# Decay rows of a gated delta rule: sixteen broadcast products, or one product and a transfer through memory

## The reference, cut to what matters

```python
beta = jax.nn.sigmoid(b)
g = -jnp.exp(A_log) * jax.nn.softplus(a + dt_bias)
g_cum = jnp.cumsum(to_chunks(g), axis=-1)
decay = jnp.exp(jnp.where(causal, g_cum[..., :, None] - g_cum[..., None, :], -jnp.inf))
m = jnp.where(strict, jnp.einsum('bhnid,bhnjd->bhnij', k_beta, kc) * decay, 0.0)
attn_intra = jnp.einsum('bhnid,bhnjd->bhnij', qc, kc) * decay
```

## Time and profile before

| | us |
|---|---|
| median of 3 runs | 906.03 |
| lowest, highest | 905.59, 906.92 |
| span of the profiled execution | 905.7 |
| TensorE busy | 894.0 (99%) |
| VectorE busy | 604.6 (67%) |
| ScalarE busy | 456.3 (50%) |
| POOL busy | 95.4 (11%) |

### The profile page before, as it was taken

One profiled execution on the slowest core, in us unless ns is written; L12 is line 12 of the kernel. 1 busy time (PEld: TensorE's weight loads), 2 busy tenths in 40 slices (PEclk: granted clock), 3 DMA queues, 4 the chain that ended last, 5 costly groups with the idle time before them and its releaser, 6 DMA issues.

```text
span 905.7 us, 12742 instructions
## 1 busy us (share of the span) xinstructions
PE 894.0 (99%) x5426; PEld 761.5 (84%) x5426; DVE 604.6 (67%) x723; ACT 456.3 (50%) x554; POOL 95.4 (11%) x94
## 2 busy tenths in 40 slices
PE   8999999999999999999999999999999999999997
PEld 8989888788888887888888878778788888888885
DVE  5899896676566557778857564655556566664665
ACT  6675564564444447555443355443355555444443
POOL 2041231100000000000126310110100000000000
PEclk9999999999999999999999999999999999999999
DMA  9654324246555543654564544344454356445531
GB/s 331 248 205 147 126 63 170 88 163 230 198 194 198 197 190 140 221 186 149 208 221 167 185 159 167 140 186 184 171 200 142 141 194 234 171 183 216 186 140 46
DMA packets 26088, 160.45 MB, mean 177 GB/s; under 512 B 3576, under 2 KB 4232, under 8 KB 8240
## 3 DMA queue, kind: packets, MB, share of 16 engines
q1 hardware_dynamic: 23616, 153.40, 46.3%
q0 software_dynamic: 2272, 6.24, 2.1%
q10 hardware_dynamic: 144, 0.00, 0.0%
HBM read 158.57 MB, written 2.63 MB: 178 GB/s over the span
## 4 chain that ended last, share of the span: by engine, by line
PE 81%; DVE 13%; ACT 3%; issue 2%; DMA 1%; POOL 0%; POOLq 0%; SPq 0%; DVEq 0%; ACTq 0%
PE banks L501 33%; PE banks L469 21%; PE banks L472 10%; DVE t_wl L1620 5%; PE banks L573 3%; PE banks L529 2%; PE banks L424 2%; PE banks L443 2%; PE banks L1019 2%; DVE t_cout L1649 2%; PE banks L412 1%; PE banks L765 1%; ACT t_wh L1139 1%; PE banks L969 1%; PE banks L1101 1%
## 5 line engine op out<-in xcount | busy, mean ns | idle before, releaser
L1620 DVE TENSOR_TENSOR t_wl<-t_raw,t_wh 128x2048 fp32r<-128x2048 f32 x136 | 312.4, 2318 | 117.0 <-ACT t_wh L1139 115.8
L469 PE MATMUL banks<-t_hx,t_wh 128*128 128x512 f32 x992 | 312.0, 396 | 0.0
L1139 ACT CAST t_wh<-t_raw 128x2048 fp32r<-128x2048 f32 x136 | 255.6, 1907 | 12.3 <-DMA t_raw<-in_W 7.6
L472 PEld LDWEIGHTS banks<-t_hx,t_wl 128*128 128x128 f32 x992 | 186.3, 188 | 43.7
L472 PE MATMUL banks<-t_hx,t_wl 128*128 128x256 f32 x992 | 194.9, 278 | 0.0
L469 PEld LDWEIGHTS banks<-t_hx,t_wh 128*128 128x128 f32 x992 | 153.3, 189 | 2.4
L501 PE MATMUL banks<-t_wh,t_hx 128*128 128x512 f32 x320 | 102.0, 395 | 0.0
L501 PEld LDWEIGHTS banks<-t_wh,t_hx 128*128 128x128 f32 x320 | 59.5, 188 | 12.7 <-issue 0.6
L501 PE MATMUL banks<-t_wl,t_hx 128*128 128x512 f32 x160 | 61.1, 390 | 0.0
L2251 POOL TENSOR_TENSOR t_st<-t_st,t_half 128x1 f32<-128x1 f32 (+1 forms) x18 | 10.6, 591 | 435.5 <-DVE t_st L1649 425.8
L1471 ACT COPY t_hold<-banks 128x512 f32<-128x512 f32 x28 | 16.4, 585 | 67.4 <-PE banks L472 56.2
(11 more groups left out here) (322 smaller groups left out, 1340.4 us busy)
## 6 DMA issues: line engine op xcount, KB each, us to landing
t_raw<-in_W SPq DMA_DIRECT2D x139, 1024.0 KB, 4.8
t_raw<-in_W SPq DMA_DIRECT2D x8, 256.0 KB, 6.5
t_raw<-in_W SPq DMA_DIRECT2D x4, 512.0 KB, 8.8
skew<-scr POOLq DMA_DIRECT2D x1, 1536.0 KB, 13.0
t_cout<-in_xT SPq DMA_DIRECT2D x4, 256.0 KB, 5.6
t_x<-in_x SPq DMA_DIRECT2D x2, 512.0 KB, 9.7
t_tab<-in_tab POOLq DMA_DIRECT2D x1, 640.0 KB, 7.4
out<-t_xt SPq DMA_DIRECT2D x2, 320.0 KB, 2.3
```

What stands on the lines that cost most here:

```text
L469: e.matmul(bank[b + c], M.wh[:, h, wk], M.hx[:, k, :, :].rearrange("p a s -> p (a s)"), start=k == 0, stop=False)
L472: m = e.matmul(bank[b + c][:, 0:S], M.wl[:, h, wk], M.hh[:, k, :], start=False, stop=k == 7)
L1139: e.copy(M.wh[:, h, :], M.raw[:, r, :]).then_inc(q.sem, q.tick(("hi", i)))
L1620: e.tensor_tensor(M.wl[:, h, :], M.raw[:, r, :], M.wh[:, h, :].bitcast(F32), ALU.subtract).then_inc(q.sem, q.tick(("lo", i)))
```

## The change

The 16 products and their four banks go. In their place TensorE makes one product with `graw` as the stationary side, 16 partitions by 128 columns, which is g_cum along the columns for each of the 16. ScalarE copies it to SBUF (`grow`, in a free part of the tile `va`), in unit 3 ahead of the first silu. POOL writes it to memory (gscr, 8 KB), waits, and loads `dU` from it, 16 rows of 512 bytes to each of 128 partitions, 1 MB; this stands behind the issue of skew and ahead of the first T loads. VectorE's 16 operations move from the end of unit 3 to unit 5, behind rn1 and ahead of the low part of unit 8, and work in place on `dU` in SBUF; they wait for the load. The product with `nstrict` (dS) moves from VectorE to POOL, behind the powers rk and rq and ahead of kd.

```diff
--- before.py
+++ after.py
@@ -307,6 +307,7 @@
             M.T = sb(pa, "T", [128, 2, 384])
             M.oh, M.ng = M.PT[0:32, 0, :], M.PT[0:8, 1, :]
             M.rb, M.rrow = M.va[0:32, 0, 0:8], M.va[0:8, 1, 0:384]
+            M.grow = M.va[0:16, 0, 128:256]
 
             def four(own, other):
                 return [own[:, 0, :], own[:, 1, :], other[:, 0:384], other[:, 384:768]]
@@ -364,7 +365,7 @@
         PE, AC, DV, PO = (Line(top.enter_context(nc.semaphore(n + "_done"))) for n in ("pe", "act", "dve", "pool"))
         raw_in = [top.enter_context(nc.semaphore(f"raw_in{i}")) for i in range(RR)]
         LD = {n: top.enter_context(nc.semaphore("in_" + n)) for n in (
-            "x0", "x1", "small", "ident", "tab", "onehot", "neg", "rbT", "scr", "skew", "post_mix", "post_mlp",
+            "x0", "x1", "small", "ident", "tab", "onehot", "neg", "rbT", "scr", "skew", "gscr", "dU", "post_mix", "post_mlp",
             "dist", "rope", "g_final", "pre", "wab", *(f"T{h}" for h in range(8)), *(f"xT{p}" for p in range(4)),
             *(f"W{i}_{p}" for i, n in PIECES.items() for p in range(n - 1)))}
         s_out = top.enter_context(nc.semaphore("out_written"))
@@ -662,15 +663,11 @@
                     e.matmul(bank[b][:, 0:16], M.triu, M.graw, start=True, stop=True)
                     e.matmul(bank[b][:, 16:32], M.ones, M.graw, start=True, stop=True).then_inc(q.sem, q.tick("sums"))
                     drain(b, DV, "kdx0")
-                    for g in range(4):
-                        b = take(("decay", g), g)
-                        opened(b)
-                        for i in range(4):
-                            s = 4 * g + i
-                            m = e.matmul(bank[b][:, i * 128:i * 128 + 128],
-                                         M.graw[:, s:s + 1].broadcast_to([128, 128]), M.triu, start=True, stop=True)
-                        m.then_inc(q.sem, q.tick(("decay", g)))
-                        drain(b, DV, ("dU", g))
+                    b = take("rows", 0)
+                    opened(b)
+                    e.matmul(bank[b][0:16, 0:128], M.graw, M.triu, start=True, stop=True).then_inc(
+                        q.sem, q.tick("rows"))
+                    drain(b, AC, "grow")
 
             c_block("z", x_in, [(AC, ("zz", t)) for t in range(2)])
             b_unit(("qk", 0), DV, ("qk", 0), to=0)
@@ -1283,6 +1280,8 @@
                     e.activation(M.cout[:, a, :], M.cin[:, a, 0:S], ACT.Copy,
                                  scale=cw[:, a, 0:1]).then_inc(q.sem, q.tick(("tap", a, 0)))
                 if u == 3:
+                    q.wait_ge(PE, "rows")
+                    e.copy(M.grow, bank[at["rows"]][0:16, 0:128]).then_inc(q.sem, q.tick("grow"))
                     silu_of(0)
                     silu_of(1)
                     silu_of(2)
@@ -1304,7 +1303,7 @@
                 q.wait_ge(PO, ("rstd", "in", c))
                 e.activation(M.zz[:, c, :], bank[at["z", c]][:], ACT.Silu, scale=M.ms[:, c:c + 1]).then_inc(
                     q.sem, q.tick(("zz", c)))
-            q.wait_ge(DV, ("dU", 3))
+            q.wait_ge(DV, "dU")
             e.activation(M.dU[:], M.dU[:], ACT.Exp).then_inc(q.sem, q.tick("dexp"))
             q.wait_ge(DV, "gc")
             e.activation(M.eg, M.gcum, ACT.Exp).then_inc(q.sem, q.tick("eg"))
@@ -1783,6 +1782,9 @@
                     q.wait_ge(q, "rn0")
                     ts(rq, rq, EPS, 64.0, ALU.add, ALU.mult, "rn1")
                     ts(rk, rk, EPS, None, ALU.add, None, "rn1")
+                    q.wait_dma(LD["dU"])
+                    for s in range(16):
+                        stt(M.dU[:, s, :], M.dU[:, s, :], M.gcum[:, s:s + 1], M.cap, ALU.subtract, ALU.min, "dU")
                     next_unit()
                 for k in range(1, 4):
                     for i in range(2):
@@ -1796,13 +1798,6 @@
                     e.tensor_copy(M.gcum, bank[b][:, 0:16]).then_inc(q.sem, q.tick("gc"))
                     q.wait_ge(q, "gc")
                     tt(M.kdx, bank[b][:, 16:32], M.gcum, ALU.subtract, "kdx0")
-                    for g in range(4):
-                        b = at["decay", g]
-                        q.wait_ge(PE, ("decay", g))
-                        for i in range(4):
-                            s = 4 * g + i
-                            stt(M.dU[:, s, :], bank[b][:, i * 128:i * 128 + 128], M.gcum[:, s:s + 1], M.cap,
-                                ALU.subtract, ALU.min, ("dU", g))
 
             q.wait_ge(PO, "rk")
             for c in range(2):
@@ -1822,8 +1817,6 @@
                 tt(M.kTa[:, 2 * u:2 * u + 2, :], halves(bank[at["qk", u]][:]), rep(M.rbc, 2), ALU.mult, ("qk", u))
 
             keys(0)
-            q.wait_ge(AC, "dexp")
-            tt(M.AT, M.dU[:], rep(M.nstrict, 16), ALU.mult, "dS")
             next_unit()
             next_unit()
             keys(1)
@@ -1862,7 +1855,7 @@
                 v = bank[at["KQ", g]][:].rearrange("p (i w n) -> p i w n", i=2, w=2)
                 a_, du = M.AT[:, s0:s0 + 3:2, :], M.dU[:, s0:s0 + 3:2, :]
                 q.wait_ge(PE, ("KQ", g))
-                q.wait_ge(q, "dS")
+                q.wait_ge(PO, "dS")
                 tt(a_, v[:, :, 0, :], a_, ALU.mult, ("AT", g))
                 tt(du, v[:, :, 1, :], du, ALU.mult, ("dq", g))
             next_unit()
@@ -2286,12 +2279,18 @@
             e.dma_start(A["scr"], M.rrow).then_inc(LD["scr"], 16)
             q.wait_dma(LD["scr"])
             e.dma_start(A["skew"], bass.AP(A["scr"].tensor, 0, [[384, 8], [0, 128], [1, 384]])).then_inc(LD["skew"], 16)
+            q.wait_ge(AC, "grow")
+            e.dma_start(A["gscr"], M.grow).then_inc(LD["gscr"], 16)
+            q.wait_dma(LD["gscr"])
+            e.dma_start(M.dU[:], bass.AP(A["gscr"].tensor, 0, [[0, 128], [128, 16], [1, 128]])).then_inc(LD["dU"], 16)
             load_T(0)
             load_T(1)
             q.wait_ge(DV, "rn1")
             for w, name in ((1, "rk"), (0, "rq")):
                 o = M.rn.rearrange("p (c w h) -> p c w h", c=2, w=2)[:, :, w, :]
                 tt(o, o, M.half[:, 0:16].rearrange("p (c h) -> p c h", c=2), ALU.pow, name)
+            q.wait_ge(AC, "dexp")
+            tt(M.AT, M.dU[:], rep(M.nstrict, 16), ALU.mult, "dS")
             q.wait_ge(AC, ("kT", 1, 2))
             q.wait_ge(AC, "kdx")
             tt(heads(M.kd), heads(M.tm[:, 0, 512:1024]), bc(M.kdx[:, 0:8], 64), ALU.mult, "kd")
@@ -2459,6 +2458,7 @@
     nc = bacc.Bacc("TRN2", target_bir_lowering=False, num_devices=1)
     A = {n: nc.dram_tensor("in_" + n, a.shape, F32, kind="ExternalInput").ap() for n, a in arrays.items()}
     A["skew"] = nc.dram_tensor("skew", [8, 128, 384], F32, kind="Internal").ap()
+    A["gscr"] = nc.dram_tensor("gscr", [16, 128], F32, kind="Internal").ap()
     A["scr"] = nc.dram_tensor("scr", [8, 384], F32, kind="Internal").ap()
     out = nc.dram_tensor("out_0", (S, D), F32, kind="ExternalOutput").ap()
     build(nc, A, out)
```

## The result

The changed kernel took 908.51 us (median of 21 runs, 906.65 to 908.81), the kernel before 906.40 (21 runs, 905.10 to 908.10). The ratio is 1.0020, 95% interval 1.0013 to 1.0026: slower by 1.2 to 2.4 us. The forecast was +0.9 us, with a range of 904.8 to 910.8.

The account below looks back on a forecast made before the run. The chain was taken to run through VectorE up to the last convolution taps, then ScalarE's exponential and unit 10's split, not TensorE. Only VectorE's idle counted, +0.9 us on the 906.03 median: 906.9, range 904.8 to 910.8.

Parts of the forecast that it names:

- late load: Rival: VectorE waits for dU's load before the sixteen operations, each us past 57.1 costing one; 910.3 to 912.2; chance 0.26.
- Part 1: TensorE, sixteen products become one: of 3.4 us it keeps 1.2 at unit 4, and is 1.6 ahead after unit 5.
- Part 2: VectorE's sixteen operations, moved behind unit 5's norm sums and reading SBUF, still take 4.14 us; floor 2.1 us less.
- Part 3: VectorE's order without the sixteen operations: idle 0.6 and 0.25 us, last taps at 63.45 instead of 62.55, +0.9 us.
- second gap: VectorE idle 0.25 us near 51.5, waiting for TensorE's unit 5 before scaling.
- Parts 4 and 5: Mask product on POOL takes 8.2 to 9.2 us, slows VectorE's low parts by a third; costed at nothing, at most 0.5.
- The prediction's rival: POOL's product holds VectorE whole, delaying low parts 10 and 11 and TensorE's third score products 3 us: 910; chance 0.06.
- Part 6: Rows through memory: write landed at 46.7, load 9.5 us more, landing at 56.2, 0.9 before VectorE asks; ends 51.6, 62.4.
- the middle price: Load of dU priced by the T loads at 49 ns a row: 9.5 us, landing 0.9 us before VectorE asks.
- The sum's base: The +0.9 us was added to the profiled span of 905.7; the median of three runs, 906.03, lay 0.3 above it.

Follow-up runs that it names:

- the first profile: The changed kernel unaltered, its first profiled execution, a run of 906.80 us; median 908.51 against 906.40 for the kernel before.
- after_filled: The changed kernel plus eight idle 128x128 products of constants in TensorE's hole in front of unit 4: 907.16 us against 906.36 before, ratio 1.0010.
- after_again: The changed kernel unaltered, timed and profiled a second time: 908.11 us against 906.41 for the kernel before, ratio 1.0018.
- ds_vector: The changed kernel with the mask product (dS) back on VectorE: 907.89 us against 906.41 for the kernel before, ratio 1.0012.
- load_late: after_filled with POOL's write and load of the rows behind the four T loads: 912.67 us against 906.33 for the kernel before, ratio 1.0067.

## Why the prediction was right, and where it was not

**The sign, the chain and the place of the cost** were right: nothing was gained from TensorE's 3.6 us and VectorE's 2.2 us, and the chain ran over the last taps, the exponential and unit 10's high part to the transposes. Ahead of them it ran over VectorE, as the prediction has it, only where the clock held; with the fall it ran over TensorE's units 4 and 5. The measured change, 1.2 to 2.4 us with 2.1 between the medians, is at the edge of the 0.2% that the forecast called no change, and more than twice its 0.9. That 908.51 still lies in the range is luck: the range reached to 910.8 for a late load, which did not happen, and had nothing in it for what did.

**Part 1** was right in its numbers: 1.2 us kept by unit 4 (36.51 - 27.56 = 8.95 against 39.17 - 29.00 = 10.17), the wait for dU's banks gone. It failed in leaving the hole that these numbers imply, 35.8 to 37.95, unpriced. It costs 1.48 us in the executions in which the clock falls. This is the term that the sum lacked, and most of the difference to the measurement: 0.75 from the first profile, and with the 1.48 of the fall 2.2, against 2.1 measured. after_filled agrees that little else is needed: without the hole it is +0.80, and the forecast, which had no term for the hole, was +0.9.

**Part 2** was right: 4.21 us by the spacing, from SBUF, for 4.14 from PSUM.

**Part 3** was right in kind and a little high: 0.51 and no second gap, for 0.6 and 0.25. Unit 5 was done just as VectorE came (no idle time at 50.06). In after_again this second gap is the one that grew to 1.46 with the slow clock. Of the hole in front of unit 8 (0.96) the prediction says nothing; there TensorE is off the chain in the first profile and it cost no time.

**Parts 4 and 5** had the wrong mechanism and, by luck, nearly the right cost. Between the Trainium skill's rule of an exclusive lock and my reading of the earlier trace rows I believed the reading, and the rule was right. I had taken the POOL products for 2.05 us each, from a row of two. Taken with the ends, the first took 1.0, the low part then its 2.2 until 126.70, and the second 0.9 behind that until 127.61: the same lock. So 2048 columns take POOL 4.4 us, not 8.2 to 9.2, and hold VectorE for as long as they last. The prediction had two errors here, contention in place of a hold and a product twice too long, and they offset each other. The prediction's rival priced the hold with 8.7 us, at +3 us; with 4.4 it is 0.1 here and 0.9 where the kernel before has no slack. The score products did not wait for POOL.

**Part 6** was right that the load is hidden, though not in its two prices: the write took 4.7 to 7.3 us to land in nine profiles and the load 5.3 to 8.1, against 4.6 and 9.5. The two errors cancel, which is luck too. In five profiles the load landed 3.2, 0.7, 0.2, 1.5 and 1.2 us before VectorE asked, where the middle price left 0.9. The estimate by the fit of the Trainium skill ("DMA: Bandwidth & Descriptors", "Anatomy of one DMA — SWDGE (gpsimd) path"), 4.4 us for the load, is short of all of these. The late load was a real rival with its price right; it did not happen.

**The sum's base.** The prediction took the span of 905.7 for a run near the median. By the 1.8 us between time and span that the later results show, it was a run of about 907.5. Since only a difference was added, the forecast did not suffer.

## What to carry to other kernels

Work taken from TensorE in a stretch that another engine paces does not become time, it becomes a hole, and a hole has a price of its own: here 1.9 us of it made the clock fall in two of four profiles and, by the clocks of the runs, probably in most executions. So compute how long TensorE will stand still before taking work from it, and fill it or move the wait. Before giving VectorE's two-input work to POOL, look at what VectorE does meanwhile: with two SBUF inputs it stops for POOL's whole instruction, and moving 2.2 us cost up to 0.9. One profile can be of the minority: find the profiled run among the times and clocks of all runs, and where it lies off the median, profile once more.

## What the runs showed of the hardware that was not expected

- A hole of 1.88 to 1.90 us on an otherwise full TensorE: in two of four profiles the granted clock went to 0.50 right behind it, for about 3.5 us, in the other two it stayed at 1.00. With eight idle products in it, it stayed at 1.00 in all five. One of the two that kept it (ds_vector) had its fall in the first stage instead (0.52 from 8 to 10 us), part of the scatter of that stage.
- In load_late TensorE stood for 6.36 us, and the clock was at 0.50 while it worked again:

```profile
66.00:68.00 2.00, 0.39 (x2) 0.40 (x3) 2.00 (x3) 0.00 (x0) 0.00 (x0) 0.50 0.00 0
68.00:70.00 2.00, 2.00 (x11) 2.00 (x11) 2.00 (x6) 0.04 (x1) 0.00 (x0) 0.50 0.67 176
```

  It cost 0.1 us over VectorE's wait at most, because the transposes waited for ScalarE anyway. The same fall costs all or nothing by who is waiting for TensorE.
- A POOL product of 128 by 2048 float32 takes 4.4 us from the end of the VectorE instruction that it has to wait for, but its row reads 5.94 to 6.75 in the five profiles that have it there: the duration of such a row contains the wait. The same holds for VectorE's low part, 6.06 us in the row and 2.16 behind POOL's end.
